# The first two tiles behind each RMS norm are multiplied un-normalised, and the token's factor is applied at their PSUM banks

## The chip, the cores and the metric

The kernel runs as one program on one core of a Trainium2 chip. The time is that of one execution on the device, in microseconds (us). The engines have short names: PE is the matrix engine (TensorE), with PEld its weight loads, DVE is VectorE, ACT is ScalarE, POOL is GpSimd and SP is the queue that issues most DMAs. Each engine runs its own instructions in order, and the engines wait for each other by semaphores. The median of three runs of the kernel before is 3070.98 us (3070.7 to 3072.57).

## What is computed

Two layers of a transformer-like network over 768 tokens of width 1024 (512 latent and 256 context tokens). Each layer is a half SwiGLU, a mixer, and another half SwiGLU. Everything is float32. All three parts begin alike, and this beginning is what the change is about:

```python
def rms_norm(x, g):
    y = xf * lax.rsqrt(jnp.mean(xf * xf, axis=-1, keepdims=True) + EPS)
    return (y * g.astype(F32)).astype(x.dtype)

def _modulate(h, g, m, k):
    return (rms_norm(h, g) * (1 + m[:, :, 3 * k + 1]) + m[:, :, 3 * k]).astype(h.dtype)

def swiglu(h, w1, w3, w2):
    return (jax.nn.silu(h @ w1) * (h @ w3)) @ w2
```

The modulation `m` differs between latent and context tokens. So the input of a product `h @ W` is, for channel d and token t, `x[d,t] * a[d] * r[t] + s[d]`, with `a` the scale (norm weight times 1 + modulation), `r` the token's factor (the inverse root of its mean square) and `s` the shift. The mixers (neighbourhood attention with a state space scan, and a linear recurrence with differential attention) use the same norm ahead of their input product.

## The kernel before

**Layout.** Channels lie on the 128 partitions, in KC = 8 chunks, and tokens along the free axis; `x` holds 8 chunks of 768 tokens. A product is cut in tiles of 128 output channels. A tile's sum lies in `G[0]` or `G[1]` in turn, two PSUM buffers of two banks each; `psum_free[s]` counts when one may be overwritten, `mm_done` counts finished tiles. In the program the tiles are numbered through: ffn0 (60 tiles), ab_in (24), ab_out (8), ffn1, ffn2, cd_in (20), cd_out (8), ffn3. An FFN runs in two halves of 22 "up" tiles (11 pairs of a gate and a hidden tile) and 8 "down" tiles.

**Precision.** Each operand is split in a high part (rounded for the matrix engine's fast float32 format) and a rest. A chunk of a tile is three products: high by high, high by rest, rest by high, each in two matmuls of 384 tokens (lines 428, 430, 432; 512 tokens in one matmul at 435 to 439 where only latent tokens run). The weights' high part is an ACT instruction (`split_hi`, line 890), the rest a DVE one (`split_lo`, line 1299), and both need the buffer `wh`/`wl` of the tile two before to be read out. The activations have `xh` and `xl` likewise.

**A norm.** There are six, numbered 0 to 5: ahead of ffn0, ab_in, ffn1, ffn2, cd_in, ffn3. While the down tiles ahead of it run, DVE adds each to `x`, ACT squares the chunk (957) and POOL adds the squares up (1893). Behind the last tile PE sums over partitions (466, 469) and runs five matmuls whose result nobody uses (475). ACT takes logarithm and exponential (972, 975), which gives `rstd`. Then for each of the 8 chunks: POOL multiplies `x` by `rstd` (1902; chunk 0 is DVE's, 1426), DVE applies scale and shift (1433, one instruction for latent and one for context tokens), ACT rounds the high part (978) and DVE takes the rest (1422). The `gemm_pair` that follows runs the first two tiles together, chunk by chunk, each as soon as its `xl` is there; the third tile's weights are split when the pair has ended.

**The order** of each engine's instructions is the order in which its function calls them. Nothing moves them later. Behind norm 2 the queue of ACT also fetches the modulation's weights (`load_mods`, 896) and the vector `scb` (`load_scb`, 913, 915) ahead of the next weight split. In the "up" part of ffn0 and ffn1, DVE, POOL and ACT compute the modulation from these (1304, 1910, 906), three channels' tiles for each pair.

## Time and profile before

| | us |
|---|---|
| median of 3 runs | 3070.98 |
| the profiled execution | 3072.22 |
| its span on the core | 3069.8 |
| PE busy in it | 2860.1 (93%) |
| DVE, ACT, POOL busy | 1474.5, 1094.9, 646.5 |

The profile shows every instruction of one execution, with its start, its duration and what ended the engine's idle time ahead of it. The span is 2.4 us shorter than the execution's own time. In the names, `tmp` are the buffers of a chunk, `raw` is a weight tile as it was loaded, and L with a number is a line of the kernel.

### The profile page before, as it was taken

How to read it: one execution, taken by the hardware profiler on the slowest of the kernel's cores; microseconds unless marked ns; L12 is line 12 of the kernel's file. 1: busy time of each engine (PE TensorE's matmuls, PEld its weight loads, DVE VectorE, ACT ScalarE, POOL GpSimd, SP SyncE). 2: the span in 40 equal slices, each digit the busy share in tenths (PEclk: the TensorE clock that was granted, in tenths of full speed). 3: DMA queues.
4: the chain of work that ended last, by engine and by line, in shares of the span. 5: the costliest groups of instructions: out<-in, count | busy, mean ns of one | idle time of the engine just before them, and what ended most of it. 6: DMA issues, size and time to landing. Idle time of an engine off the chain costs nothing.

```text
span 3069.8 us, 40707 instructions
## 1 busy us (share of the span) xinstructions
PE 2860.1 (93%) x15782; PEld 2658.3 (87%) x15782; DVE 1474.5 (48%) x1848; ACT 1094.9 (36%) x1465; POOL 646.5 (21%) x336
## 2 busy tenths in 40 slices
PE   5899999989977797999999899999998987899999
PEld 5899999978965687999999899999997855668887
DVE  7874366254556836652564422222225557543332
ACT  3342144125455333431342243112212657454221
POOL 4441144120013714430342300000022113110000
PEclk8999999999999898999999999999999989899999
DMA  6443144111210012441342112211211210123233
GB/s 259 155 147 124 57 158 151 63 43 52 72 38 1 1 42 103 157 154 58 130 157 93 37 62 62 75 55 61 72 51 56 62 55 1 42 75 101 91 96 103
DMA packets 67666, 258.70 MB, mean 84 GB/s; under 512 B 7424, under 2 KB 8576, under 8 KB 66944
## 3 DMA queue, kind: packets, MB, share of 16 engines
q1 hardware_dynamic: 50016, 192.58, 18.9%
q10 hardware_dynamic: 17568, 65.02, 6.0%
q8 instruction: 53, 0.87, 0.1%
q14 instruction: 29, 0.24, 0.0%
HBM read 255.47 MB, written 2.10 MB: 84 GB/s over the span
## 4 chain that ended last, share of the span: by engine, by line
PE 81%; DVE 10%; ACT 2%; issue 2%; POOL 1%; DMA 0%; DVEq 0%; ACTq 0%; POOLq 0%
PE G L428 20%; PE G L432 20%; PE G L430 20%; PE G L435 5%; PE G L439 5%; PE G L437 5%; DVE tmp L1433 2%; DVE B L1304 1%; DVE xl L1422 1%; DVE sL L1632 1%; PE NP L691 1%; PE G L782 1%; DVE wl L1299 1%; DVE sL L1623 1%; PE NP L600 1%
## 5 line engine op out<-in xcount | busy, mean ns | idle before, releaser
L890 ACT ACTIVATE wh<-raw 128x1024 fp32r<-128x1024 f32 (+1 forms) x300 | 338.8, 1129 | 1578.0 <-PE G L432 1285.0
L428 PE MATMUL G<-xh,wh 128*128 128x384 f32 x2752 | 711.3, 339 | 73.4 <-DVE xl L1422 47.7
L430 PE MATMUL G<-xl,wh 128*128 128x384 f32 x2752 | 704.7, 337 | 0.0
L432 PE MATMUL G<-xh,wl 128*128 128x384 f32 x2752 | 704.0, 336 | 0.0
L1299 DVE TENSOR_TENSOR wl<-raw,wh 128x1024 fp32r<-128x1024 f32 (+1 forms) x300 | 429.4, 1431 | 406.8 <-ACT wh L890 406.0
L428 PEld LDWEIGHTS G<-xh,wh 128*128 128x128 f32 x2752 | 500.3, 190 | 87.6 <-issue 40.9
L430 PEld LDWEIGHTS G<-xl,wh 128*128 128x128 f32 x2752 | 503.0, 190 | 0.0
L432 PEld LDWEIGHTS G<-xh,wl 128*128 128x128 f32 x2752 | 501.9, 190 | 0.0
L1910 POOL TENSOR_TENSOR mraw<-mraw,scb 128x1024 f32<-128x1024 f32 x120 | 315.0, 2625 | 598.7 <-DVE B L1304 598.7
L428 PE MATMUL G<-hh,wh 128*128 128x384 f32 x1056 | 268.0, 334 | 0.0
L432 PE MATMUL G<-hh,wl 128*128 128x384 f32 x1056 | 267.8, 334 | 0.0
L430 PE MATMUL G<-hl,wh 128*128 128x384 f32 x1056 | 267.8, 334 | 0.0
L1364 DVE SCALAR_TENSOR_TENSOR x<-G,modG,x 128x256 f32<-128x256 f32 x112 | 49.1, 480 | 440.0 <-PE G L432 440.0
L1304 DVE SCALAR_TENSOR_TENSOR B<-mraw,scb 128x1024 f32<-128x1024 f32 x120 | 235.2, 1960 | 0.0
L435 PE MATMUL G<-xh,wh 128*128 128x512 f32 (+1 forms) x544 | 207.6, 391 | 8.2 <-DVE xl L1422 4.0
L439 PE MATMUL G<-xh,wl 128*128 128x512 f32 (+1 forms) x544 | 205.2, 387 | 0.0
L437 PE MATMUL G<-xl,wh 128*128 128x512 f32 (+1 forms) x544 | 205.1, 387 | 0.0
L1332 DVE TENSOR_TENSOR tmp<-tmp,G 128x768 f32<-128x768 f32 x66 | 63.0, 954 | 295.4 <-PE G L432 294.4
L432 PEld LDWEIGHTS G<-hh,wl 128*128 128x128 f32 x1056 | 190.6, 188 | 0.0
L428 PEld LDWEIGHTS G<-hh,wh 128*128 128x128 f32 x1056 | 190.6, 188 | 0.0
L430 PEld LDWEIGHTS G<-hl,wh 128*128 128x128 f32 x1056 | 190.6, 188 | 0.0
L906 ACT ACTIVATE mraw<-mraw 128x1024 f32<-128x1024 f32 x120 | 126.3, 1053 | 34.4 <-ACT mraw L906 24.0
(308 smaller groups left out, 3104.3 us busy)
## 6 DMA issues: line engine op xcount, KB each, us to landing
raw<-in_w SPq DMA_DIRECT2D x176, 512.0 KB, 3.6
mraw<-in_wmn ACTq DMA_DIRECT2D x120, 512.0 KB, 4.4
raw<-in_w SPq DMA_DIRECT2D x64, 704.0 KB, 4.1
raw<-in_abin SPq DMA_DIRECT2D x24, 512.0 KB, 3.5
raw<-in_cdin SPq DMA_DIRECT2D x20, 512.0 KB, 3.6
mini<-in_wmn SPq DMA_DIRECT2D x9, 512.0 KB, 14.8
gmini<-in_wmn SPq DMA_DIRECT2D x2, 2048.0 KB, 22.0
raw<-in_about SPq DMA_DIRECT2D x8, 512.0 KB, 3.6
```

The lines of the kernel that those rows point to most:

```text
L428: pe.matmul(bank(h), W, tokens(rh, h), start=(k == 0), stop=False)
L430: pe.matmul(bank(h), W, tokens(rl, h), start=False, stop=False)
L432: mm = pe.matmul(bank(h), L, tokens(rh, h), start=False, stop=(k == nk - 1))
L435: pe.matmul(G[slot][:, a:b], W, rh[:, k, a:b], start=(k == 0), stop=False)
L437: pe.matmul(G[slot][:, a:b], W, rl[:, k, a:b], start=False, stop=False)
L439: mm = pe.matmul(G[slot][:, a:b], L, rh[:, k, a:b], start=False, stop=(k == nk - 1))
L890: act.activation(wh[slot][:, 0:nk * P], raw[slot][:, 0:nk * P], ACT.Copy).then_inc(hi_done, 1)
L906: act.activation(mraw[:, j, :], mraw[:, j, :], ACT.Copy, accum_out=M[:, bass.ds(it * 3 + (24 + j), 1), 1:2].rearrange("p a s -> p (a s)")) ...
L1299: dve.tensor_tensor(wl[slot][:, 0:nk * P], raw[slot][:, 0:nk * P], wh[slot][:, 0:nk * P].bitcast(F32), ALU.subtract).then_inc(lo_done, 1)
L1304: return dve.scalar_tensor_tensor(B67[:], tile, 1.0, scv[:, s, :], ALU.mult, ALU.mult, accum_out=out)
L1332: dve.tensor_tensor(by_block(hf[:, 0:T]), by_block(g1s[:, 0:T]), from_banks(G[1], 0, T), ALU.mult).then_inc(psum_free[1], 1)
L1910: pool.tensor_tensor(mraw[:, j, :], mraw[:, j, :], scb[:, 1, :], ALU.mult).then_inc(mod_prod, 1)
```

## The change

For norms 1 to 5 (norm 0 has no product running ahead of it):

- DVE multiplies each chunk of `x` by the scale as soon as the down tile ahead has been added (`ub`), ACT rounds it and DVE takes the rest; this is `unnormed(n)`. Two more columns, the shift for latent and for context tokens, stand behind the 768 tokens of each chunk.
- PE takes the first tile wholly, then the second, on these operands (`gemm_unnormed`), in matmuls of 512 and 258 columns. The norm's sums over partitions stand behind the first tile's third chunk. The five matmuls of line 475 are gone.
- At the bank, DVE copies the two shift columns and multiplies the tokens by `rstd`; the shift's product is added later (`scale_bank` and its callers).
- The norm itself, for all later tiles, runs meanwhile. POOL's multiplication is gone: DVE takes `x * a * rstd` in one instruction for each kind of token, ACT adds the shift as its bias while it rounds, and DVE adds the shift and takes the rest in one. This holds for norm 0, too. The third tile waits for each chunk.
- The modulation of the next norm is prepared ahead of the down tiles. In ffn1, `load_scb` stands behind the first hidden chunk, and the modulation's work starts one pair later.

In the diff, `gemm_unnormed` and what follows it is PE's, the `norm` with `between` ACT's, and from `scale_bank` on it is DVE's (the part with `nn` stands behind the addition of a down tile).

```diff
+            def gemm_unnormed(t, n, segs):
+                uh, ul = (hxh, hxl) if n in (2, 5) else (xh, xl)
+                e = NLAT if segs is SEGS else NLAT // 2
+                ns = segs[-1][1]
+                for s in range(2):
+                    weights_ready(t + s, s, t // 2)
+                    for k in range(KC):
+                        if s == 0:
+                            pe.wait_ge(u_ready, 8 * (n - 1) + k + 1)
...
+                        parts = ((0, e, 0), (512, 512 + ns + 2 - e, e))
+                        for a, b, o in parts:
+                            pe.matmul(G[s][:, a:b], W, uh[:, k, o:o + b - a], start=(k == 0), stop=False)
...
+                        if s == 0 and k == 2:
+                            norm_sums(n, segs)
...
-                    if h == 0:
-                        gemm_pair(b, xh, xl, segs, xn)
-                    with pe.Fori(int(h == 0), FH) as i:
+                    elif h == 0:
+                        gemm_unnormed(b, n, segs)
+                        gemm(b + 2, 0, b // 2 + 1, KC, xh, xl, gsegs, xn)
+                        gemm(b + 3, 1, b // 2 + 1, KC, xh, xl, gsegs)
+                        done = 2
...
             def norm(n, segs, between):
-                    act.wait_ge(aff_done, 8 * n + j + 1)
-                    act.activation(xh[:, j, 0:ns], yn[j % 2][:, 0:ns], ACT.Copy).then_inc(xn_hi, 1)
+                    act.wait_ge(v_ready, 8 * n + j + 1)
+                    if n in IN_PLACE:
+                        if j < KC - 1:
+                            act.wait_ge(u_read, 7 * IN_PLACE.index(n) + j + 1)
...
+                        ins = act.activation(xh[:, j, a:b], vn[j % 4][:, a:b], ACT.Identity, bias=M[:, c0 + j, c:c + 1])
+                    ins.then_inc(xn_hi, 1)
+                    between(j)
+            def between_up(n, segs):
+                def between(j):
+                    if j == 0:
+                        split_hi(FIRST_TILE[n] + 2, 0, FIRST_TILE[n] // 2 + 1, KC)
+                    if j == 3:
+                        act.wait_ge(u_gate, LATE_UP.index(n) + 1)
+                        for a, b, c in segs:
+                            ins = act.activation(g1u[:, a:b], g1u[:, a:b], ACT.Silu, bias=pb[:, 0, c:c + 1])
+                        ins.then_inc(psum_free[0], 1)
...
+            def scale_bank(s, n, ns, out):
+                dve.wait_ge(mm_done, FIRST_TILE[n] + s + 1)
+                dve.tensor_copy(pb[:, s, :], G[s][:, T:TX])
+                for src, a, b in late_tokens(G[s], ns):
+                    ins = dve.tensor_tensor(out[:, a:b], src, rstd[:, a:b], ALU.mult)
+                return ins
+            def scale_gate(n, segs):
+                scale_bank(0, n, segs[-1][1], g1u).then_inc(u_gate, 1)
+                split_lo(FIRST_TILE[n] + 2, 0, KC)
+            def scale_hidden(n, segs):
+                chain(scale_bank(1, n, segs[-1][1], hfu))
+                dve.wait_ge(psum_free[0], FIRST_TILE[n] // 2 + 1)
+                for a, b, c in segs:
+                    ins = dve.scalar_tensor_tensor(hfu[:, a:b], hfu[:, a:b], pb[:, 1, c:c + 1], g1u[:, a:b], ALU.add, ALU.mult)
+                ins.then_inc(psum_free[1], 1)
...
+                        if nn is not None:
...
+                                ins = dve.tensor_scalar(ub[j % 2][:, a:b], x[:, j, a:b], modA[:, nn, j, c:c + 1], None, ALU.mult)
+                            ins.then_inc(u_scaled, 1)
...
-                chain(dve.tensor_tensor(vn[0][:, 0:ns], x[:, 0, 0:ns], rstd[:, 0:ns], ALU.mult))
+                        ins = dve.scalar_tensor_tensor(vn[j % 4][:, a:b], x[:, j, a:b], modA[:, n, j, c:c + 1], rstd[:, a:b],
+                                                       ALU.mult, ALU.mult)
```

Where the instructions stand now, at three places. On PE, from the last down tile of ffn0 to the first tiles of ab_in. Before: the sums, the five matmuls, then the pair, chunk by chunk of both tiles (`wh_57` and `wh_58` are the weights of the two).

```order
L466 MATMUL NP<-ssq,con 128x512
L466 MATMUL NP<-ssq,con 128x256
L469 MATMUL NP<-sq_66,con 128x512
L469 MATMUL NP<-sq_66,con 128x256
L475 MATMUL G<-con 128x512 x5
L428 MATMUL G<-xh,wh_57 128x384 x2
L430 MATMUL G<-xl,wh_57 128x384 x2
L432 MATMUL G<-xh,wl_59 128x384 x2
```

After: the first tile's third chunk ends, the sums follow, and the same tile's fourth chunk goes on.

```order
L507 MATMUL G<-xh,wh_57 128x512
L507 MATMUL G<-xh,wh_57 128x258
L509 MATMUL G<-xl,wh_57 128x512
L509 MATMUL G<-xl,wh_57 128x258
L511 MATMUL G<-xh,wl_59 128x512
L511 MATMUL G<-xh,wl_59 128x258
L488 MATMUL NP<-ssq,con 128x512
L488 MATMUL NP<-ssq,con 128x256
L491 MATMUL NP<-sq_66,con 128x512
L491 MATMUL NP<-sq_66,con 128x256
L507 MATMUL G<-xh,wh_57 128x512
L507 MATMUL G<-xh,wh_57 128x258
```

The sums moved from ahead of the product into its first tile, and the second tile no longer takes turns with it.

On DVE, at norm 1, from the last weight rest on. Before (`tmp_61`, `tmp_62` hold x times rstd, `tmp_63`, `tmp_64` the modulated chunk):

```order
L1299 TENSOR_TENSOR wl_60<-raw_56,wh_58 128x1024
L1318 TENSOR_TENSOR M<-M,par 128x48
L1386 SCALAR_TENSOR_TENSOR modA<-M,par 128x16
L1395 TENSOR_SCALAR modG<-M 128x16
L1426 TENSOR_TENSOR tmp_61<-x,rstd 128x768
L1433 TENSOR_SCALAR tmp_63<-tmp_61,modA,M 128x512
L1433 TENSOR_SCALAR tmp_63<-tmp_61,modA,M 128x256
L1433 TENSOR_SCALAR tmp_64<-tmp_62,modA,M 128x512
L1433 TENSOR_SCALAR tmp_64<-tmp_62,modA,M 128x256
L1422 TENSOR_TENSOR xl<-tmp_63,xh 128x768
```

After (`pb` is the copy of the shift's columns, `vT` the first tile's output, `wl_59` the third tile's weights):

```order
L1590 SCALAR_TENSOR_TENSOR tmp_61<-x,modA,rstd 128x512
L1590 SCALAR_TENSOR_TENSOR tmp_61<-x,modA,rstd 128x256
L1590 SCALAR_TENSOR_TENSOR tmp_62<-x,modA,rstd 128x512
L1590 SCALAR_TENSOR_TENSOR tmp_62<-x,modA,rstd 128x256
L1581 SCALAR_TENSOR_TENSOR xl<-tmp_61,M,xh 128x512
L1581 SCALAR_TENSOR_TENSOR xl<-tmp_61,M,xh 128x256
L1468 COPY pb<-G 128x2
L1470 TENSOR_TENSOR vT<-G,rstd 128x512
L1470 TENSOR_TENSOR vT<-G,rstd 128x256
L1492 TENSOR_SCALAR vT<-vT,pb 128x512
L1492 TENSOR_SCALAR vT<-vT,pb 128x256
L1403 TENSOR_TENSOR wl_59<-raw_55,wh_57 128x1024
```

The first bank's work and the third tile's weight rest now stand between chunk 0's rest and chunk 2, in the middle of the norm.

On ACT, from the end of norm 2 into ffn1. Before:

```order
L978 ACTIVATE xh<-tmp_64 128x768
L896 DMA mraw<-in_wmn 128x1024 x3
L913 DMA scb<-in_ccb 128x2048
L915 ACT_TABLE_LOAD
L915 ACTIVATE scb<-scb 128x2048
L890 ACTIVATE wh_57<-raw_55 128x1024
L924 ACTIVATE tmp_61<-G 128x768
L890 ACTIVATE wh_58<-raw_56 128x1024
```

After (`sq_65` holds the first hidden chunk):

```order
L1064 ACTIVATE xh<-tmp_64,M 128x256
L951 DMA mraw<-in_wmn 128x1024 x3
L945 ACTIVATE wh_58<-raw_56 128x1024
L995 ACTIVATE hh<-sq_65 128x768
L968 DMA scb<-in_ccb 128x2048
L970 ACTIVATE scb<-scb 128x2048
L945 ACTIVATE wh_57<-raw_55 128x1024
L979 ACTIVATE tmp_61<-G 128x768
```

The second weight split and the first chunk's high part moved ahead of the fetch of `scb`; what is queued behind that fetch is now the fifth tile's weights, not the third's.

## Rows read from the trace of the kernel before

**Rows 1.** PE's timeline, norm 1: start, us, line, operation [idle before <-releaser].

```profile
631.14 1.45 PE L466 MATMUL NP<-ssq,con 128*128 128x512 f32 x4
633.54 1.56 PE L469 MATMUL NP<-sq,con 128*128 128x512 f32 x4 [0.95 <-ACT sq L957]
...
645.07 0.98 PE L428 MATMUL G<-xh,wh 128*128 128x384 f32 x2 [5.69 <-DVE xl L1422]
...
668.80 0.62 PE L428 MATMUL G<-xh,wh 128*128 128x384 f32 x2 [1.43 <-DVE wl L1299]
```

**Rows 2.** DVE's timeline in ab_in: copies of two tiles in a row.

```profile
677.46 0.96 DVE L1498 COPY vT<-G 128x768 f32<-128x768 f32 x1 [6.71 <-PE G L432]
...
685.77 0.96 DVE L1498 COPY vT<-G 128x768 f32<-128x768 f32 x1 [5.94 <-PE G L432]
```

**Rows 3.** timeline of DVE at norm 1: weight rest, chunks.

```profile
632.52 1.22 DVE L1299 TENSOR_TENSOR wl<-raw,wh 128x1024 fp32r<-128x1024 f32 x1
...
638.32 2.57 DVE L1426 TENSOR_TENSOR tmp<-x,rstd 128x768 f32<-128x768 f32 x1 [4.16 <-ACT rstd L975]
...
657.71 2.20 DVE L1433 TENSOR_SCALAR tmp<-tmp,modA,M 128x512 f32<-128x512 f32 x2
...
660.89 0.87 DVE L1433 TENSOR_SCALAR tmp<-tmp,modA,M 128x512 f32<-128x512 f32 x2
```

**Rows 4.** timeline of PE, norms 2, 3, 5: first sum, third tile.

```profile
1156.54 1.45 PE L466 MATMUL NP<-ssq,con 128*128 128x512 f32 x4
...
1200.05 1.00 PE L428 MATMUL G<-xh,wh 128*128 128x384 f32 x2 [7.30 <-DVE wl L1299]
...
1734.91 1.45 PE L466 MATMUL NP<-ssq,con 128*128 128x512 f32 x4
...
1773.36 0.62 PE L428 MATMUL G<-xh,wh 128*128 128x384 f32 x2 [2.23 <-ACT tmp L924]
...
2689.16 1.02 PE L466 MATMUL NP<-ssq,con 128*128 128x512 f32 x2
...
2716.49 0.50 PE L435 MATMUL G<-xh,wh 128*128 128x512 f32 x1 [2.38 <-ACT tmp L924]
```

**Rows 5.** ACT's timeline behind norm 2: scb, its Silu, fifth tile's weights.

```profile
1188.51 0.46 ACTq L913 DMA_DIRECT2D scb<-in_ccb  x1
...
1195.80 1.91 ACT L915 ACTIVATE scb<-scb 128x2048 f32<-128x2048 f32 x1 [5.52 <-DMA scb<-in_ccb]
...
1219.27 1.06 ACT L890 ACTIVATE wh<-raw 128x1024 fp32r<-128x1024 f32 x1 [3.61 <-PE G L432]
```

**Rows 6.** timeline of DVE at norm 0: first and last work of the norm.

```profile
52.92 0.96 DVE L1426 TENSOR_TENSOR tmp<-x,rstd 128x768 f32<-128x768 f32 x1
...
74.64 1.96 DVE L1422 TENSOR_TENSOR xl<-tmp,xh 128x768 fp32r<-128x768 f32 x2
```

**Rows 7.** timeline of PE at the third tile of ab_out.

```profile
1106.50 0.62 PE L428 MATMUL G<-xh,wh 128*128 128x384 f32 x2 [1.45 <-DVE wl L1299]
```

**Rows 8.** DVE's groups by shape: xcount | busy us, mean ns | idle.

```profile
L1364 DVE SCALAR_TENSOR_TENSOR x<-G,modG,x 128x256 f32<-128x256 f32 x112 | 49.1, 480 | 440.0 <-PE G L432 440.0
...
L1371 DVE SCALAR_TENSOR_TENSOR x<-G,modG,x 128x512 f32<-128x512 f32 x24 | 18.0, 751 | 100.2 <-PE G L439 100.2
```

**Rows 9.** timeline of ACT at norm 1: the high part of one chunk.

```profile
659.95 0.84 ACT L978 ACTIVATE xh<-tmp 128x768 fp32r<-128x768 f32 x1 [2.33 <-DVE tmp L1433]
```

**Rows 10.** the page's DMA issues: KB each, median us from issue to landing.

```profile
raw<-in_w SPq DMA_DIRECT2D x176, 512.0 KB, 3.6
...
raw<-in_w SPq DMA_DIRECT2D x64, 704.0 KB, 4.1
```

**Rows 11.** timeline of DVE behind norm 5: the fifth tile's weight rest.

```profile
2725.00 1.23 DVE L1299 TENSOR_TENSOR wl<-raw,wh 128x1024 fp32r<-128x1024 f32 x1 [5.76 <-ACT wh L890]
```

**Rows 12.** stretches: us, busy by engine, PEclk, DMA share, GB/s.

```profile
668.80:672.00 3.20, 3.20 (x18) 3.20 (x19) 1.95 (x2) 0.00 (x0) 0.00 (x0) 1.00 0.48 164
...
2718.00:2720.00 2.00, 2.00 (x6) 1.54 (x5) 1.24 (x2) 0.49 (x1) 0.00 (x0) 0.50 0.42 152
```

More of the change, by code:

```diff
@@ L324, in group, with unnormed, shift, late_tokens @@
             return [j in g for g in MINI_GROUPS].index(True)
+        IN_PLACE = (1, 3, 4)
+        LATE_UP = (2, 3, 5)
+        FIRST_TILE = {1: BASE["ab_in"], 2: BASE["ffn1"], 3: BASE["ffn2"], 4: BASE["cd_in"], 5: BASE["ffn3"]}
+        def unnormed(n):
+            return (hxh, hxl) if n in (2, 5) else (xh, xl)
+        def shift(n):
+            c0 = (n // 3) * NMT + 3 * KC * (n % 3)
+            return M[:, c0:c0 + KC, :]
+        def late_tokens(buf, ns):
+            e = NLAT if ns == T else NLAT // 2
+            return ((buf[:, 0:e], 0, e), (buf[:, 512:512 + ns - e], e, ns))
         def by_block(ap):
@@ L933, in pair @@
                         sum_mod(now, 0, more)
+                first = 0
+                if unnormed_first:
+                    split_hi(b + 3, 1, b // 2 + 1, KC)
+                    act.wait_ge(psum_free[1], b // 2 + 1)
+                    act.activation(hh[:, 0, 0:ns], hfu[:, 0:ns], ACT.Copy).then_inc(h_hi, 1)
+                    first = 1
                 if mods is None:
-                    with act.Fori(0, FH - 1) as i:
+                    with act.Fori(first, FH - 1) as i:
                         pair(i, KC)
@@ L939, in up @@
                     return
+                if unnormed_first:
+                    act.wait_ge(h_ready, hb + 1)
+                    load_scb(2)
                 end = mods + FH - 2
                 last = end in (19, 39)
-                pair(0, KC, now=mods)
-                with act.Fori(1, FH - 2) as i:
-                    pair(i, KC, late=i + (mods - 1), now=i + mods)
-                pair(FH - 2, KC, late=end - 1, now=end, more=not last)
-                pair(FH - 1, look, late=end, late_more=not last)
+                pair(first, KC, now=mods)
+                with act.Fori(first + 1, FH - 2 + first) as i:
+                    pair(i, KC, late=i + (mods - 1 - first), now=i + (mods - first))
+                if first:
+                    pair(FH - 1, look, late=end - 1, now=end, more=not last)
+                    sum_mod(end, 1, not last)
+                    sum_mod(end, 2, not last)
+                else:
+                    pair(FH - 2, KC, late=end - 1, now=end, more=not last)
+                    pair(FH - 1, look, late=end, late_more=not last)
             def square(j, n, chunk, ns):
@@ L971, in norm @@
+                            act.activation(uh[:, j, 0:ns], ub[j % 2][:, 0:ns], ACT.Copy).then_inc(u_hi, 1)
+            def norm(n, segs, between):
+                ns = segs[-1][1]
+                c0 = (n // 3) * NMT + 3 * KC * (n % 3)
                 act.wait_ge(norm_sum, n + 1)
-                act.activation(sq[0][:, 0:ns], NP[:, 0:ns], ACT.Ln, bias=eps[:, 0:1], scale=1.0 / D
-                               ).then_inc(norm_ln, 1)
-                act.wait_ge(norm_ln, n + 1)
+                chain(act.activation(sq[0][:, 0:ns], NP[:, 0:ns], ACT.Ln, bias=eps[:, 0:1], scale=1.0 / D))
@@ L1111, in ssd_act @@
                 act.wait_ge(gn_sum, 4)
[L1112 to L1113 removed]
+                chain(act.activation(lng[:], NP[:, 0:T], ACT.Ln, bias=eps[:, 0:1], scale=1.0 / 512))
                 act.activation(rsg[:], lng[:], ACT.Exp, scale=-0.5).then_inc(gn_rs, 1)
@@ L1482, in conv @@
                     ins.then_inc(conv_done, 1)
-                for c in range(AB_IN_T):
+                for c in range(1, AB_IN_T):
                     t, s = AB + c, c % 2
@@ L1707, in conv @@
                     ins.then_inc(conv_done, 1)
-                for c in range(CD_IN_T):
+                for c in range(1, CD_IN_T):
                     t, s = CD + c, c % 2
```

322 lines of the change are left out of this document (188 added, 134 removed).

## The prediction, made before the changed kernel had run

> **What bounds the kernel now.** PE is busy for 93% of the span, so the time lies in its matmuls and in the stretches where it waits. I went first to PE's timeline around a norm, then to DVE's, which PE names as its releaser. At norm 1 the last down tile ends at 631.14; the third tile of ab_in begins at 668.80, 37.66 us later [rows 1]. Two tiles lie between, and a tile costs 8.31 us, the distance of two copies in a row in the steady product [rows 2]. So 37.66 - 16.62 = 21.0 us of each such norm are not product. PE sums for about 2.7 us of them, and waits for the chain Ln, Exp, x times rstd, scale and shift, high part, rest. Then it is paced by that chain: chunk follows chunk at 3.18 us (657.71 to 660.89), where PE needs 2.08 for both tiles. DVE's scale and shift takes 2.20 us there, and 0.87 on the last chunk, when POOL has no multiplication left [rows 3]. After the pair the third tile's weights are late: their releaser is `wl` or the gate's bank [rows 1, 4]. The same distance is 43.51 us at norm 2, 38.45 at norm 3 and 27.33 at norm 5 (512 tokens) [rows 4]; norm 4 repeats norm 1 to 0.1 us. At norm 2 the third tile waits 7.30 us more, since ACT sits behind the load of `scb` (issue 1188.51, Silu 1195.80) [rows 5]. Norm 0 ends on DVE at 76.60, after 23.7 us [rows 6].
>
> **What it becomes, with t = 0 at the end of the last down tile.** I follow norm 1 and give the others by what differs.
>
> PE no longer waits at t = 0. The first tile's weights were split a tile earlier, and its chunks 0 to 6 were rounded under the down tiles. Chunk 7 needs the addition (1.4), the scaling (0.9, as the 0.87 above), the weight rest (1.22) and its own rest (about 1.0): ready at 4.6, wanted after 10. Each down tile gets some 2.2 us more of DVE and 0.8 of ACT, under 8.3 us or more of PE; this costs nothing. An exception is ab_out's third tile, which already waits for its weights' rest [rows 7]: the scaling stands ahead of that, **+1.0 us**. Tile one takes 8.3 + 2.7 for the sums (two groups of four passes, 1.45 and 1.56 us with their drains [rows 1]): it ends at 11.0, tile two at 19.3.
>
> The norm. Its second group of sums starts at 3.1 + 1.3 = 4.4. Between the same point and DVE's first chunk lie 638.32 - 633.54 = 4.78 us before [rows 1, 3], so DVE starts at 9.2. From here DVE decides. A chunk is now two pairs of scalar_tensor_tensor, of 512 and 256 tokens: 0.751 + 0.480 us [rows 8], 1.23 for a pair; two in a row overlap a little, and I take 1.07, with 1.23 as the other bound. That is 2.14 us a chunk instead of 3.18, with no POOL in it. ACT needs two instructions for 0.84 us of work [rows 9], an estimated 0.95, and keeps up.
>
> - Norm 1: ACT must not overwrite chunk 0 before tile two has read it, at 11.0 + 1.0 + 0.2. High part until 13.2, rest until 14.3. The bank (copy 0.1, product 1.0, shift 0.9) and the third tile's weight rest 1.22 make 3.2: 17.5. Then 13 pairs, 13.9: 31.4. Two small instructions 0.4, the second bank and the fourth tile's rest 3.2: the fourth tile begins at **35.1**. PE could have begun it at about 32.5, so DVE still bounds. Before it was 37.66 + 8.31 = 45.97. **-10.9 us**, and the same at norm 4, **-10.8**.
> - Norm 3: the bank's shift is left to ACT, so 2.4 instead of 3.2; 13 pairs end at 30.6. Second bank with the gate's product 2.3, weight rest 1.2: 34.2 against 38.45 + 8.31 = 46.8. **-12.6.** ACT gives the gate's bank back at 23.3, which delays the third tile by 4, but it still ends before DVE does.
> - Norm 2: its operands lie elsewhere, so the high part need not wait; DVE's first rest ends at 12.5, the fourth tile begins at 32.4 and ends at 40.7. The first hidden chunk's rest ends at 33.3, and only then is `scb` fetched. Its landing is not 7.3 us as before, when 1.5 MB were issued right ahead of it: 512 KB take 3.6 us and 704 KB 4.1 [rows 10], from which I estimate 4.9 for 1 MB. Silu 1.9, high part 1.05, rest 1.2: the fifth tile begins at 42.6, a wait of 1.9. Before it began at about 1219.1, 62.6 us behind 1156.54 [rows 4, 5]. **-20.0**; with 7.3 us of landing and a cold start behind the wait it is -15.9.
> - Norm 5: 512 tokens, 0.67 us each instead of a pair, and two matmuls of 256 and 258 columns instead of one, about 5.8 us a tile. The same steps give the fourth tile at 23.5. Before, the third tile ended about 1.3 us ahead of 2725.00 [rows 11], at 34.5. **-11.0.**
> - Norm 0: 14 steps of 1.07 until the last chunk goes to ACT, 67.9 instead of 74.7 (52.92 + 15.0; before, ACT takes it where DVE's last rests begin [rows 6]). All that follows, `scb` included, comes that much earlier: **-6.8.**
>
> The sum is 1.0 - 6.8 - 10.9 - 20.0 - 12.6 - 10.8 - 11.0 = -71.1.
>
> **The clock.** In the row of 2716.49, PE starts the third tile after 2.38 us of idleness, and the granted clock is 0.50 (the 1.2 GHz level) in 2718 to 2720; at norm 1, after 1.43 us behind the weights, it stays at 1.00, 2.4 GHz [rows 4, 12]. The fourth tile will start after 2.1 to 2.6 us of idleness in five places. A cold start costs about 1.7 us: that third tile took 2716.49 to about 2723.7, 7.2 us where its work is 8.31 x 512 / 768 = 5.5 [rows 2, 4, 11]. I charge three of the five, **+5.0**; none or all five move this by -5 and +3.4.
>
> So -66.1 us. From the profiled execution of 3072.22 this gives 3006.1; that execution lay 1.2 us above the median, so I forecast **3005 us**.
>
> A rule speaks against the change. DVE's single-input instruction took 0.87 us for 768 tokens and a two-input one with a scalar takes 1.07 to 1.23 [rows 3, 8]: fusing the product with rstd gives up a fast form. The Trainium skill ("SBUF — State Buffer", "Who interferes with whom") has the other side: DVE's fast single-input form and POOL's reads exclude each other. The rows agree, 2.20 us beside POOL and 0.87 without. By the page alone, the old form without POOL would cost 0.95 + 0.87 + 0.95 a chunk, more than the new 2.14.
>
> **Rivals.**
> 1. *The chunk chain is slower than two pairs.* If each rest waits for ACT's round trip (1.07 + 0.95 + 1.07 and two hand-overs of 0.1, 3.3 us a chunk), seven chunks cost 1.15 more each in six norms: +48, **3053 us**. For it: today's chain waits like this, 3.18 us a chunk. Against: another chunk's pair stands between the two, and four buffers instead of two.
> 2. *PE is cold through the third tiles.* At norms 1 and 4 that tile gets a chunk each 2.14 us for 1.04 us of work. If the clock falls there and behind every wait, all five fourth tiles and norm 2's fifth start cold: **3011 us**, within the range.
> 3. *Slower: the 258-column matmuls.* In the fast float32 format no row shows a width that is no multiple of 128. If such a piece ran at the rate of the sums' plain float32, where 768 columns take about 1.3 us, it would take 0.43 us instead of 0.11. In two tiles of five norms these are 240 pieces of it, 24 a tile: +77, **3082 us**. It decides from about 0.39 us a piece. Against: 256, 384 and 512 columns all cost one column per cycle of 2.4 GHz.
> 4. *The change does not do what it says*, because the fourth tile waits for the same chain that the first waited for. This is half true already, and priced: from t = 0 to the fourth tile there are 35.1 us with 24.9 of product. It would only cancel the gain if DVE had 11 us more in the chain, 0.8 us on each of 13 pairs; no row points there. **3071 us.**
>
> **How the numbers follow.** The forecast's own case holds 0.72, from 2994 (no cold start, a little less on DVE) to 3020 (1.23 us a pair: 16 x 0.16 in six norms is 14). Rival 1 has 0.07, rival 2 0.09, rival 3 0.05, rival 4 0.03, and 0.04 is left for something between. The range 2994 to 3030 holds the forecast, rival 2 and part of the rest, about 0.83. A measurement of this kernel can tell 0.2% (6 us) from no change. Faster: 0.91; same: 0.03, rival 4; slower: 0.06, rival 3 and some unseen cost.
>
> **What the profile of the changed kernel would show.** PE without idle from the last down tile to the end of tile two, 19.3 us; the fourth tile 35.1 us (norm 2: 32.4, norm 3: 34.2, norm 5: 23.5) behind it, with DVE's `wl` as its releaser; pairs of DVE at 1.07 us each; the fifth tile of ffn1 after a wait of about 2 us. I am wrong if the 258-column pieces stand out, if chunks follow each other at over 2.5 us in tile three, if down tiles begin to show gaps, or if the fifth tile of ffn1 waits over 5 us.

## The result, and the profile after the change

The changed kernel takes 3054.4 us (median of four runs, 3051.2 to 3056.7) beside 3071.7 us for the kernel before: 0.995 of the time, 95% interval 0.993 to 0.996. It is faster by 17 us where 66 were forecast, and lies outside the range of 2994 to 3030. The profiled execution took 3056.2 us, with a span of 3054.4.

The page of the changed kernel, the busy times of its engines:

```profile
PE 2886.8 (95%) x15780; PEld 2688.9 (88%) x15780; DVE 1538.8 (50%) x2035; ACT 1084.7 (36%) x1514; POOL 569.8 (19%) x294
```

PE was busy for 2860.1 us before and is for 2886.8 now. The matmuls of the warm-up are gone and nothing large was added to PE, yet it is busy 27 us longer. That is the first sign: time went from waiting into the matmuls.

The places that the forecast spoke of came out as forecast. PE's timeline of the changed kernel (start, duration, instruction, and in brackets the idle time before it with its releaser), at norms 1 to 5:

```profile
635.07 1.45 PE L488 MATMUL NP<-ssq,con 128*128 128x512 f32 x4
...
666.96 0.61 PE L450 MATMUL G<-xh,wh 128*128 128x384 f32 x2 [1.93 <-DVE wl L1403]
...
1160.08 1.45 PE L488 MATMUL NP<-ssq,con 128*128 128x512 f32 x4
...
1189.63 0.62 PE L450 MATMUL G<-xh,wh 128*128 128x384 f32 x2 [1.97 <-DVE wl L1403]
...
1202.06 0.61 PE L450 MATMUL G<-xh,wh 128*128 128x384 f32 x2 [2.06 <-DVE wl L1403]
...
1731.83 1.45 PE L488 MATMUL NP<-ssq,con 128*128 128x512 f32 x4
...
1763.52 0.62 PE L450 MATMUL G<-xh,wh 128*128 128x384 f32 x2
...
2301.87 1.45 PE L488 MATMUL NP<-ssq,con 128*128 128x512 f32 x4
...
2334.41 1.01 PE L450 MATMUL G<-xh,wh 128*128 128x384 f32 x2 [2.17 <-DVE wl L1403]
...
2681.34 1.02 PE L488 MATMUL NP<-ssq,con 128*128 128x512 f32 x2
...
2702.72 0.50 PE L457 MATMUL G<-xh,wh 128*128 128x512 f32 x1 [0.30 <-DVE wl L1403]
```

L488, the first sum, stands behind three chunks of the first tile, 3.17 us behind the end of the last down tile (2.16 with 512 tokens). So t = 0 is 631.90 at norm 1 (631.14 before, [rows 1]), and the fourth tile begins at 666.96, 35.1 us later: the forecast was 35.1. At norm 2 it is 32.7 (forecast 32.4), at norm 3 34.9 (34.2), at norm 4 35.7 (35.1), at norm 5 23.5 (23.5). The releaser is DVE's `wl`, as forecast, except at norm 3, where the fourth tile follows the third without a wait. The fifth tile of ffn1 (1202.06) is later, 45.2 instead of 42.6.

Now lay the starting points of the norms beside each other. Norm 1 starts at 631.90 against 631.14 in [rows 1], though norm 0 ended some 7 us earlier; norm 2 at 1156.9 against 1156.54 in [rows 4], though norm 1 gave its 11 us. What each norm gives, the steady product between two norms takes back. There the groups of PE's instructions by shape (busy us, mean ns of one) read, before the change:

```profile
L428 PE MATMUL G<-xh,wh 128*128 128x384 f32 x2752 | 711.3, 339 | 73.4 <-DVE xl L1422 47.7 <-DVE wl L1299 23.4 <-ACT tmp L924 2.2
L428 PE MATMUL G<-hh,wh 128*128 128x384 f32 x1056 | 268.0, 334 | 0.0
```

and in the changed kernel, where the same matmul is L450:

```profile
L450 PE MATMUL G<-xh,wh 128*128 128x384 f32 x2624 | 694.5, 346 | 39.4 <-DVE wl L1403 18.8 <-DVE xl L1581 14.3 <-issue 6.0
L450 PE MATMUL G<-hh,wh 128*128 128x384 f32 x1056 | 267.9, 334 | 0.0
```

A piece that reads `xh` takes 346 ns in the mean instead of 339; one that reads `hh` takes 334 in both. The change made the rows of `xh` and `xl` two floats longer (770) and left those of `hh`. Windows of PE's activity (busy time with the matmuls counted, granted clock, share of DMA, GB/s), before:

```profile
1900.00:1920.00 20.00, 20.00 (x117) 1.00 0.21 68
2760.00:2780.00 20.00, 20.00 (x90) 1.00 0.30 105
```

and after:

```profile
1900.00:1920.00 20.00, 20.00 (x114) 1.00 0.21 72
2760.00:2780.00 20.00, 20.00 (x88) 1.00 0.32 87
```

PE is fully busy in all four at the full clock, and gets 2 to 3% fewer matmuls done. The timeline shows where: single chunks. Before the change, the first product of two chunks in a row:

```profile
1905.55 0.51 PE L428 MATMUL G<-xh,wh 128*128 128x384 f32 x2
...
1906.59 0.51 PE L428 MATMUL G<-xh,wh 128*128 128x384 f32 x2
```

and after, of three:

```profile
1905.30 0.51 PE L450 MATMUL G<-xh,wh 128*128 128x384 f32 x2
...
1906.34 0.53 PE L450 MATMUL G<-xh,wh 128*128 128x384 f32 x2
...
1907.43 0.52 PE L450 MATMUL G<-xh,wh 128*128 128x384 f32 x2
```

A chunk of three products took 1.04 us each time; now it takes 1.04 and then 1.09. A row of 770 floats is 3080 bytes, so every second chunk begins 8 bytes off a multiple of 16. Over a whole stretch (the 150 us behind the first half of ffn1, the starts of some 850 matmuls, clock 1.00) the eight chunks of a tile take 8.587 us instead of 8.320. L450 counts 2624 pieces, 16 a tile: 164 tiles of 768 tokens, 44 us. The 62 tiles of 512 tokens take 5.574 us instead of 5.440, 8 us more. Together this is a little more than the 49 us that are missing.

### The profile page after: what moved, and what is told of

It reads as the page before. It is cut to its first block, busy times and chain, and to the rows that moved or that the text cites. A ratio compares the mean times of both kernels' runs of the same rounds, so it can differ in the third digit from the quotient of the medians.

```text
span 3054.4 us, 40954 instructions
## 1 busy us (share of the span) xinstructions
PE 2886.8 (95%) x15780; PEld 2688.9 (88%) x15780; DVE 1538.8 (50%) x2035; ACT 1084.7 (36%) x1514; POOL 569.8 (19%) x294
## 4 chain that ended last, share of the span: by engine, by line
PE 83%; DVE 9%; ACT 2%; issue 2%; POOL 1%; DMA 0%; DVEq 0%; ACTq 0%; POOLq 0%
PE G L450 20%; PE G L452 20%; PE G L454 20%; PE G L461 5%; PE G L459 5%; PE G L457 5%; DVE B L1408 1%; DVE xl L1581 1%; DVE sL L1795 1%; DVE wl L1403 1%; PE NP L742 1%; DVE tmp L1590 1%; PE G L846 1%; PE G L833 1%; PE NP L651 1%
## 5 line engine op out<-in xcount | busy, mean ns | idle before, releaser
L450 PE MATMUL G<-xh,wh 128*128 128x384 f32 x2624 | 694.5, 346 | 39.4 <-DVE wl L1403 18.8
L452 PE MATMUL G<-xl,wh 128*128 128x384 f32 x2624 | 689.2, 344 | 0.0
L454 PE MATMUL G<-xh,wl 128*128 128x384 f32 x2624 | 686.3, 343 | 0.0
L1403 DVE TENSOR_TENSOR wl<-raw,wh 128x1024 fp32r<-128x1024 f32 (+1 forms) x300 | 416.8, 1389 | 401.6 <-ACT wh L945 400.6
L450 PEld LDWEIGHTS G<-xh,wh 128*128 128x128 f32 x2624 | 485.2, 191 | 49.8 <-DVE wl L1403 19.9
L452 PEld LDWEIGHTS G<-xl,wh 128*128 128x128 f32 x2624 | 487.9, 191 | 0.0
L454 PEld LDWEIGHTS G<-xh,wl 128*128 128x128 f32 x2624 | 487.0, 190 | 0.0
L450 PE MATMUL G<-hh,wh 128*128 128x384 f32 x1056 | 267.9, 334 | 0.0
L450 PEld LDWEIGHTS G<-hh,wh 128*128 128x128 f32 x1056 | 190.6, 188 | 0.0
```

The costliest lines, as they stand in the source:

```text
L450: pe.matmul(bank(h), W, tokens(rh, h), start=(k == 0), stop=False)
L452: pe.matmul(bank(h), W, tokens(rl, h), start=False, stop=False)
L454: mm = pe.matmul(bank(h), L, tokens(rh, h), start=False, stop=(k == nk - 1))
L1403: dve.tensor_tensor(wl[slot][:, 0:nk * P], raw[slot][:, 0:nk * P], wh[slot][:, 0:nk * P].bitcast(F32), ALU.subtract).then_inc(lo_done, 1)
```

## Experiments

Three theories. **A**: what costs is where the streamed operand's rows start. **B**: what costs is a row length other than 768 floats. **C**: what costs is the changed work itself, the 258-column pieces, more instructions on DVE and ACT, the clock. The last runs ask which part of the change gives the gain. Times are medians, beside runs of the kernel before on the same chip (3071.5 to 3072.9 us).

### Rows of 772 floats in the changed kernel

```diff
-TX = T + 2
+TX = T + 4
...
-                dve.tensor_copy(pb[:, s, :], G[s][:, T:TX])
+                dve.tensor_copy(pb[:, s, :], G[s][:, T:T + 2])
```

> The changed kernel with rows of xh and xl 772 floats long instead of 770 (3088 bytes, a multiple of 16); the two extra columns, the pieces of 258 columns and all else stay. Theory A, the start of the rows: in the changed kernel every second chunk of xh and xl begins 8 bytes off a multiple of 16, and a chunk of three products takes 1.09 us there against 1.05 for its neighbour and 1.04 before the change. A tile loses 0.2 us, some 184 tiles of 768 tokens and the 512-token ones lose 45 to 50 us. Then this kernel takes 3054 - 47 = 3007 us (3002 to 3014), and PE's 20-us windows hold 117 to 118 matmuls again. Theory B, the pitch: any row that is not 768 floats long is slower. Then it stays at 3054. Theory C, the changed work itself (the 258-column pieces, more instructions of DVE and ACT beside PE, the clock): 3054 too.

Measured: 3029.7 us (0.986 of before, 0.984 to 0.987). Chunks take 1.039 to 1.070 us, 8.426 a tile. B and C fall as they stood: two floats more in a row, never read, make the kernel 25 us faster. A's own range, 3002 to 3014, was missed: its first form, multiples of 16 bytes, is too lenient, as half the loss stays. In the tiles of 512 tokens nearly all of it stays, 5.566 us each against 5.574 with rows of 770.

### Rows of 770 floats in the kernel before

```diff
-        xh = at("xh", [P, KC, T], w, F32R); w += KC * T
+        xh = at("xh", [P, KC, T + 2], w, F32R); w += KC * (T + 2)
... (the same for xl; buffers that lie inside the two move with them)
```

> The kernel before, with nothing changed but the length of the rows of xh and xl, 770 floats instead of 768 (the two more are never read). Theories A (start of the rows) and B (pitch): every tile fed by xh and xl loses 0.2 us as in the changed kernel, 3071 + 45 to 50 = 3119 us (3112 to 3126), windows of 113 to 114 matmuls in place of 117 to 118. Theory C (the changed work): 3071.

Measured: 3121.9 us, 49.2 above the kernel before (1.016, 1.014 to 1.018). This is the direct measurement of the step that the forecast left out. Chunk by chunk the two kernels agree: 1.058, 1.087, 1.061, 1.103, 1.047, 1.093, 1.049, 1.090 us here, and 1.057, 1.087, 1.061, 1.102, 1.048, 1.092, 1.049, 1.090 in the changed kernel. Nothing else of the change slows a steady tile, and C has no part in it.

### The kernel before with its buffers shifted by 8, 16, 32 and 64 bytes

The rows stay 768 floats; only the start moves. The shift of 8 bytes (16: `4` for `2`):

```diff
-        xh = at("xh", [P, KC, T], w, F32R); w += KC * T
+        xh = at("xh", [P, KC * T + 8], w, F32R)[:, 2:KC * T + 2].rearrange("p (k t) -> p k t", k=KC); w += KC * T + 8
(the same for xl)
```

> The kernel before, rows of xh and xl 768 floats long as they were, but both buffers begin 2 floats (8 bytes) later, so that every chunk begins 8 bytes off a multiple of 16. Theory A (start of the rows): all eight chunks of a tile cost what every second one does in the changed kernel, 8 x 0.05 = 0.4 us a tile; with 184 tiles and the 512-token ones twice the loss of the changed kernel, 3071 + 80 to 100 = 3161 us (3145 to 3180). Theory B (pitch) and theory C (the changed work): 3071.

> The kernel before, rows of 768 floats, both buffers begin 4 floats (16 bytes) later. Theory A (start of the rows, counted in 16 bytes), B and C: 3071 (3068 to 3075). If what matters is a start counted in 32 or 64 bytes, it is as slow as the one with 8 bytes, 3145 to 3180, and the changed kernel with rows of 772 floats keeps its slow chunks.

For 32 and 64 bytes each buffer is 16 floats longer and the slice begins at 8 or 16:

> The kernel before, rows of 768 floats, both buffers begin 8 floats (32 bytes) later, so that every chunk begins 32 bytes off a multiple of 64. If the start counts in 32 bytes: 3071 (3068 to 3076), a chunk 1.04 us. If it counts in 64 bytes: a chunk of 1.05 to 1.07 us as at 16 bytes off, 3090 to 3115.

> The kernel before, rows of 768 floats, both buffers begin 16 floats (64 bytes) later. If only the start modulo 64 bytes counts: 3071 (3068 to 3075), a chunk 1.04 us. If the shift itself, or the bank that a row falls in, counts: slower, as the shift by 16 bytes was (3115).

As each buffer also grew, `xl` starts 32 bytes further than `xh` modulo 64 in the first two, which their descriptions don't say. Measured, with the time of a chunk in the same stretch:

| shift | `xh`, `xl` start modulo 64 | chunk, 768 tokens, us | chunk, 512 tokens, us | time, us | ratio (95%) |
|---|---|---|---|---|---|
| none | 0, 0 | 1.040 | 0.680 | 3071.7 | |
| 8 bytes | 8, 40 | 1.093 | 0.700 | 3146.5 | 1.024 (1.022 to 1.026) |
| 16 bytes | 16, 48 | 1.067 | 0.700 | 3115.1 | 1.014 (1.012 to 1.016) |
| 32 bytes | 32, 32 | 1.047 | 0.707 | 3090.6 | 1.006 (1.004 to 1.007) |
| 64 bytes | 0, 0 | 1.047 | 0.703 | 3088.7 | 1.005 (1.004 to 1.007) |

PE's timeline with the shift of 8 bytes, the first product of two chunks in a row, 1.09 us apart:

```profile
1520.98 0.53 PE L428 MATMUL G<-xh,wh 128*128 128x384 f32 x2
...
1522.07 0.53 PE L428 MATMUL G<-xh,wh 128*128 128x384 f32 x2
```

And with the shift of 32 bytes, in the tiles of 512 tokens, 0.71 us apart (0.68 unshifted):

```profile
2766.23 0.40 PE L435 MATMUL G<-xh,wh 128*128 128x512 f32 x1
...
2766.93 0.40 PE L435 MATMUL G<-xh,wh 128*128 128x512 f32 x1
```

That the start matters holds, and B falls: the rows have 768 floats in all of them. In the tiles of 768 tokens a chunk pays 0.053 us at 8 bytes and 0.027 at 16. The shift of 16 bytes fell between the times that A foresaw for its two forms (3071, or 3145 to 3180). The expectation for 64 bytes (3071) was missed: 0.007 us a chunk remains there, as much as at 32 bytes. So a start modulo 64 isn't the whole rule, and "only the start modulo 64 counts" is refuted. The tiles of 512 tokens, whose matmuls read 512 tokens in one run and not three blocks of 128, say so more clearly: they pay 0.020 to 0.027 us a chunk for every shift, and 32 bytes cost them more than 8. What orders these prices, and the last 0.007 us, is open.

### The weights shifted by 16 bytes

The tiles fed by `hh` had kept 1.04 us in every kernel, but in all of them `hh` and the weights had moved together. So the distance between streamed rows and loaded weights could have been the cause.

```diff
-        wh = [at(f"wh{s}", [P, FH * P], w + s * FH * P, F32R) for s in range(2)]; w += 2 * FH * P
+        wh = [at(f"wh{s}", [P, FH * P + 8], w + s * (FH * P + 8), F32R)[:, 4:FH * P + 4] for s in range(2)]; w += 2 * (FH * P + 8)
(the same for wl)
```

> The kernel before, xh, xl, hh and hl where they were, but both weight buffers wh and wl (what TensorE loads as weights) begin 16 bytes later. Theory A' (the start of the operand that streams): its address has not moved, a chunk stays at 1.04 us in tiles fed by xh and in those fed by hh, 3071 us (3068 to 3077), unless the load itself slows. Theory R (what counts is the distance between the streamed rows and the weights that are loaded beside them): tiles fed by hh are now as far off as those fed by xh were when these were shifted by 16 bytes; both kinds take 1.06 to 1.07 us a chunk, and the time is 3071 + 45 + 20 = 3135 us (3110 to 3145).

Measured: 3101.6 us (1.010, 1.008 to 1.011), below the range of the one theory and above that of the other. The group of the first product with `hh`:

```profile
L428 PE MATMUL G<-hh,wh 128*128 128x384 f32 x1056 | 269.7, 336 | 0.0
```

336 ns instead of 334, with `hh` on its old place: where the weights lie costs something too. In tiles fed by `xh` a chunk takes 1.051 us in the mean. It isn't even: tiles whose weights lie in the first pair of buffers (16 bytes off a multiple of 64) space their matmuls at some 176 ns, those of the second pair (48 bytes off) at 174, next to 173 before. By distance alone both should be slow, since the shift by 16 bytes had `xh` 16 and `xl` 48 bytes off with both slow. So distance alone falls, and the loaded operand's own place counts. In tiles of 768 tokens it counts less than the streamed one's. In those of 512 tokens a chunk takes 0.694 us with either pair, beside 0.680.

### Rows of 784 floats in the changed kernel

3136 bytes are 49 x 64. A table product had to move to make room.

```diff
-TX = T + 2
+TX = T + 16
...
-        t2b = small("t2b", [P, NLAT])
+        t2b = at("t2b", [P, NLAT], H + 38 * NLAT); fw[0] += P
```

> The changed kernel with rows of xh and xl 784 floats long (3136 bytes, 49 x 64), so that every chunk begins on a multiple of 64 bytes; to make room the table product of the rotary step lies in another buffer. Rows of 770 floats gave 3054, of 772 3030. Theory A', the start of the rows counted in 32 or 64 bytes (a chunk takes 1.04 us on a multiple of 64, 1.07 at 16 bytes off it in every chunk of the kernel before shifted by 16 bytes, 1.09 at 8 bytes off): all chunks take 1.04 again and what the wider rows cost, 0.24 us in each of some 184 tiles and about 5 in those of 512 tokens, is back: 3054 - 49 = 3005 us (3000 to 3011), the forecast. Theory B (pitch: any row that is not 768 floats long is slower): between 3025 and 3054. Theory C (part of the missing gain is in the changed work itself): 3015 to 3030, with windows of 117 to 118 matmuls and the remainder at the norms.

Measured: **3015.3 us** (3012.3 to 3017.2; 0.981 of before, 0.980 to 0.983), better than both kernels, but above the 3000 to 3011 of theory A' and at the lower end of what theory C foresaw. The tiles tell the two apart. PE's timeline at the norms (L489 is the first sum):

```profile
627.54 1.45 PE L489 MATMUL NP<-ssq,con 128*128 128x512 f32 x4
...
659.41 0.62 PE L451 MATMUL G<-xh,wh 128*128 128x384 f32 x2 [0.72 <-DVE wl L1404]
...
1143.64 1.45 PE L489 MATMUL NP<-ssq,con 128*128 128x512 f32 x4
...
1705.52 1.45 PE L489 MATMUL NP<-ssq,con 128*128 128x512 f32 x4
...
1737.19 0.62 PE L451 MATMUL G<-xh,wh 128*128 128x384 f32 x2 [0.92 <-DVE wl L1404]
...
2265.72 1.45 PE L489 MATMUL NP<-ssq,con 128*128 128x512 f32 x4
...
2640.41 1.02 PE L489 MATMUL NP<-ssq,con 128*128 128x512 f32 x2
```

With 3.13 us taken off each (2.16 for the last), the norms start at 624.4, 1140.5, 1702.4, 2262.6 and 2638.2, and the span ends at 3012.9. Stage by stage against the kernel before:

| from, to | forecast, without clock | rows of 770 | rows of 784 |
|---|---|---|---|
| start to norm 1 | -6.8 | +0.8 | -6.7 |
| norm 1 to norm 2 | -9.9 | -0.4 | -9.3 |
| norm 2 to norm 3 | -20.0 | -6.6 | -16.5 |
| norm 3 to norm 4 | -12.6 | -1.0 | -10.8 |
| norm 4 to norm 5 | -10.8 | -2.7 | -7.6 |
| norm 5 to the end | -11.0 | -5.4 | -6.0 |

A tile takes 8.347 us, 0.027 above 8.320, which leaves 4 to 5 us in all. The stage behind norm 5 gains hardly more than with 770 (-6.0 and -5.4). The fourth tile begins where it should, so the tiles of 512 tokens are still slow: they take 5.56 us each, beside 5.44 before and 5.57 with 770, some 7 us over the 62 of them, though every row starts on a multiple of 64 bytes. So what is missing lies in the steady tiles and not in the changed work, which theory C had named.

### The two columns in a buffer of their own

Rows of 768 floats again; the shift's columns are multiplied by themselves.

```diff
-                        parts = ((0, e, 0), (512, 512 + ns + 2 - e, e))
+                        parts = ((0, e, 0), (512, 512 + ns - e, e))
...
+                        pe.matmul(G[s][:, sa:sb], W, shh[:, k, :], start=False, stop=False)
+                        pe.matmul(G[s][:, sa:sb], W, shl[:, k, :], start=False, stop=False)
...
+                        pe.matmul(G[s][:, sa:sb], L, shh[:, k, :], start=False, stop=False)
```

> The changed kernel with rows of xh and xl 768 floats long, as before the change; the two columns for the shift stand in a buffer of their own and are multiplied by three more matmuls of 2 columns on each chunk of the first two tiles behind norms 1 to 5 (24 a tile, 240 in all), and the pieces of 258 columns become 256. Theory A'' (each operand's own start): all chunks of the other tiles take 1.04 us again, so the 49 us of the 770-float rows come back, and the 8 to 9 us that the rows of 784 floats still miss against the forecast as well, less what the 2-column matmuls cost: between 0.03 and 0.10 us each, 0.7 to 2.4 us a tile, of which the second tile's share is partly under the chain of DVE that bounds: 5 x 1 to 5 x 4 = 5 to 20. 3005 + 5 to 20 = 3010 to 3025 us. If something else in the changed work slowed the tiles, it stays near 3030 or above.

Measured: 3016.6 us (0.982, 0.981 to 0.984), no different from rows of 784. Steady tiles are back at 1.04 us a chunk, those of 512 tokens at 0.68, and the 20-us window of the latter holds 90 matmuls. PE's timeline of the first tile behind norm 1 and of the fourth:

```profile
624.65 0.51 PE L510 MATMUL G<-xh,wh 128*128 128x512 f32 x2
624.99 0.17 PE L511 MATMUL G<-shh,wh 128*128 128x2 f32 x1
...
626.02 0.52 PE L510 MATMUL G<-xh,wh 128*128 128x512 f32 x2
...
662.62 0.75 PE L452 MATMUL G<-xh,wh 128*128 128x384 f32 x2 [1.98 <-DVE wl L1409]
```

A chunk takes 626.02 - 624.65 = 1.37 us instead of 1.04, so each matmul of 2 columns costs 0.11, a little over what was expected. The fourth tile begins 38.0 us behind the last down tile instead of 35.1. With 3.0 more at each of norms 1, 3 and 4, 1.7 at norm 5 and nothing at norm 2, where the fifth tile begins no later than with rows of 784, this is 10.7: taken off 3016.6, it gives 3006, next to the forecast of 3005. The two columns have a price either way, and the forecast had them for nothing.

### The fused chain alone

The kernel before, with the new form of a norm's chunk and nothing hidden:

```diff
-                        ins = dve.tensor_scalar(yn[j % 2][:, a:b], vn[j % 2][:, a:b], modA[:, n, j, c:c + 1],
-                                                M[:, c0 + j, c:c + 1], ALU.mult, ALU.add)
-                    ins.then_inc(aff_done, 1)
+                        ins = dve.scalar_tensor_tensor(tmp[j % 4][:, a:b], x[:, j, a:b], modA[:, n, j, c:c + 1], rstd[:, a:b],
+                                                       ALU.mult, ALU.mult)
+                    ins.then_inc(v_ready, 1)
...
-                pool.wait_ge(rstd_ready, n + 1)
-                for j in range(1, KC):
...
```

> The kernel before with one part of the change alone: the norm's chunk is two pairs of scalar_tensor_tensor (x times scale times rstd, then shift minus high part) in four buffers, and GpSimd multiplies nothing; every tile still waits for the norm, rows stay 768 floats. Theory F (the chain is the larger part): at norm 1 the chain of 16 pairs of 1.07 us starts 7.2 us behind the last down tile and ends at 24.5, the third tile's weight rest 1.2 follows, so that the third tile begins at 26 to 28 instead of 37.66: -10 us at each of norms 1 to 4, -5 at norm 5 (512 tokens, 0.67 us a piece), -7 at norm 0, together -52: 3071 - 52 = 3019 us (3012 to 3030). Theory H (the hiding of the two tiles is the larger part, as the change is described): the chain gives the 1.05 us a chunk on seven chunks only until PE's own 2.08 us a chunk bounds, -5 at each norm, about 3045 us.

Measured: 3028.7 us (0.986, 0.984 to 0.988), 43.6 below the kernel before and already 26 below the changed kernel. DVE's timeline at norm 1:

```profile
633.50 1.14 DVE L1436 SCALAR_TENSOR_TENSOR tmp<-x,modA,rstd 128x512 f32<-128x512 f32 x2
634.56 1.14 DVE L1427 SCALAR_TENSOR_TENSOR xl<-tmp,M,xh 128x512 fp32r<-128x512 f32 x2
635.62 1.14 DVE L1436 SCALAR_TENSOR_TENSOR tmp<-x,modA,rstd 128x512 f32<-128x512 f32 x2
```

and PE's:

```profile
622.85 1.45 PE L466 MATMUL NP<-ssq,con 128*128 128x512 f32 x4
...
652.23 0.61 PE L428 MATMUL G<-xh,wh 128*128 128x384 f32 x2 [1.42 <-DVE wl L1302]
```

A pair takes 1.06 us, a chunk 2.12 instead of 3.18. The third tile begins 29.4 us behind the last down tile (26 to 28 were expected) instead of 37.66 ([rows 1]). Norm 0 ends 7.6 us earlier, at 69.0 instead of 76.6. The chain is the larger part of the gain, as theory F said.

### The hiding alone, with the old chain

The kernel with rows of 784 floats, with the product on GpSimd, scale and shift, and rest as before:

```diff
-                        ins = dve.scalar_tensor_tensor(vn[j % 4][:, a:b], x[:, j, a:b], modA[:, n, j, c:c + 1], rstd[:, a:b],
-                                                       ALU.mult, ALU.mult)
-                    ins.then_inc(v_ready, 1)
+                        ins = dve.tensor_scalar(yn[j % 2][:, a:b], vn[j % 2][:, a:b], modA[:, n, j, c:c + 1],
+                                                M[:, c0 + j, c:c + 1], ALU.mult, ALU.add)
+                    ins.then_inc(aff_done, 1)
```

> The changed kernel with aligned rows (784 floats, 3015 us), but with the norm's chunks as before the change: the product with rstd on GpSimd, scale and shift, high part and rest, in two buffers each. The hiding of the first two tiles stays, the fused chain goes. Chunks follow each other at 3.18 us again instead of 2.12. Theory F: the fourth tile begins 8 x 1.05 = 8.4 us later at norms 1 to 4, 5 later at norm 5, and norm 0 ends 7 later: 3015 + 46 = 3061 us (3052 to 3070), hardly below the kernel before. Theory H: the longer chain is partly hidden under the two tiles, 3035 us.

Measured: 3048.5 us (0.992, 0.991 to 0.994), 33 above the kernel with the fused chain, between the two theories. DVE's timeline at norm 1 and PE's first sum and fourth tile:

```profile
651.28 0.86 DVE L1591 TENSOR_SCALAR tmp<-tmp,modA,M 128x512 f32<-128x512 f32 x2
...
653.12 2.19 DVE L1591 TENSOR_SCALAR tmp<-tmp,modA,M 128x512 f32<-128x512 f32 x2
...
656.28 2.18 DVE L1591 TENSOR_SCALAR tmp<-tmp,modA,M 128x512 f32<-128x512 f32 x2
```

```profile
635.63 1.45 PE L491 MATMUL NP<-ssq,con 128*128 128x512 f32 x4
...
671.84 0.62 PE L453 MATMUL G<-xh,wh 128*128 128x384 f32 x2 [0.77 <-DVE wl L1404]
```

Chunks follow at 3.16 us. But while DVE takes the first tile from its bank, GpSimd multiplies ahead, and one chunk's scale and shift is done in 0.86 us. Also, the fused chain stands still for 2.34 us at its first chunk, until ACT may overwrite what the first tile reads, and the slower one does not. So the fourth tile comes at 39.3 us, 4.3 later and not 8.4. Norm 0, where nothing hides the chain, ends 7.6 us later, as expected. Together: the chain gives 44 us alone and 33 on top of the hiding; the hiding gives 24 alone and 13 on top of the chain. Both figures of the hiding still carry the some 10 us that rows of 784 cost.

### The product on DVE, unfused

```diff
+                    chain(dve.tensor_tensor(vn[j % 2][:, 0:ns], x[:, j, 0:ns], rstd[:, 0:ns], ALU.mult))
...
-                    pool.tensor_tensor(vn[j % 2][:, 0:ns], x[:, j, 0:ns], rstd[:, 0:ns], ALU.mult
-                                       ).then_inc(v_ready, 1)
```

> The kernel before with one step moved: the product x times rstd of a norm's chunk is done by DVE itself (0.95 us) and not by GpSimd; scale and shift, high part and rest stay as they were, in two buffers. Theory P (DVE's scale and shift takes 2.20 us only because GpSimd multiplies beside it, 0.87 without): a chunk is 0.95 + 0.87 + 0.95 = 2.8 us on DVE instead of 3.18, if the round trip of ACT lies beside the next chunk's product: 8 x 0.4 = 3 us less at norms 0 to 4, less at norm 5: 3071 - 15 = 3056 us (3050 to 3062), against 3029 for the fused form. Theory Q (it is slow for another reason, or the round trip of ACT sets the pace): a chunk is 0.95 + 2.20 + 0.95 = 4.1 us, 3071 + 5 x 7 = 3106 us (3095 to 3115).

Measured: 3052.1 us (0.994, 0.992 to 0.995). DVE's timeline at norm 1, one chunk and the product of the next:

```profile
645.13 0.96 DVE L1429 TENSOR_TENSOR tmp<-x,rstd 128x768 f32<-128x768 f32 x1
646.12 0.87 DVE L1431 TENSOR_SCALAR tmp<-tmp,modA,M 128x512 f32<-128x512 f32 x2
...
647.90 0.96 DVE L1429 TENSOR_TENSOR tmp<-x,rstd 128x768 f32<-128x768 f32 x1
```

Theory P holds: with GpSimd silent the scale and shift takes 0.87 us on every chunk, and a chunk 647.90 - 645.13 = 2.77 us, the sum that the forecast had worked out. Taking work from GpSimd onto a DVE that is the bound made the kernel 19 us faster. Still, two fused pairs (2.12) beat three cheap instructions (2.77).

## Why the forecast was wrong, point by point

- **The step that failed: wider rows.** The change part names 258-column pieces, and rival 3 looked at them as a width. The same edit makes the rows 770 floats long for every tile that reads `xh` or `xl`, and that had no term. The forecast left the steady tiles at their old 8.31 us; they took 8.587, and the price, measured alone in the kernel before, is 49.2 us. Forecast 3005 + 49 = 3054, the measured time. That this meets to the microsecond is partly luck, since two smaller terms below were off, one up and one down.
- **Rival 3** did not happen: the 258-column pieces take 283 ns in the mean, with their drains, where those of 256 took 279 to 281. The right kind of cost was weighed at the wrong place. It looked at the width of an instruction and not at where its operand starts.
- **The norms** were right: fourth tile at 35.1, 32.7, 34.9, 35.7 and 23.5 us against 35.1, 32.4, 34.2, 35.1 and 23.5. A pair took 1.06 us against 1.07. With rows of 784 the stage up to norm 1 gave -6.7 against -6.8, the next, with norm 1 and ab_out, -9.3 against -9.9. One reading was loose and did no harm: the third tile of norm 2 waited 7.30 us in all, not 7.30 more than the others; the sum used the distance of 43.51, which is right. **Rivals 1 and 4** are out: a chunk takes 2.12 us, not 3.3, and the fourth tile is not 11 us late.
- **The landing of `scb`** was mis-sized, as the two rows of ACT's queue and ACT in the changed kernel show:

```profile
1190.48 0.33 ACTq L968 DMA_DIRECT2D scb<-in_ccb  x1
1197.80 1.92 ACT L970 ACTIVATE scb<-scb 128x2048 f32<-128x2048 f32 x1 [8.48 <-DMA scb<-in_ccb]
```

  It takes 7.3 us, as in [rows 5], and not the 4.9 estimated from smaller transfers. The fifth tile of ffn1 began at 45.2 instead of 42.6. The other bound, -15.9, is near the -16.5 that this stage gave with rows of 784, but it held a cold start behind that wait, which did not come; the slow stretch lay in the fourth tile instead.
- **The clock.** Three cold starts were charged to fourth tiles. Windows in the changed kernel, in order of time: the fourth tiles of norms 1 and 2, the fifth of norm 2, the fourth of norm 4 (us, PE busy with its matmuls counted, granted clock, DMA share, GB/s):

```profile
668.00:672.00 4.00, 4.00 (x16) 0.57 0.74 232
1190.00:1194.00 4.00, 4.00 (x16) 0.58 0.72 244
1202.00:1206.00 4.00, 3.94 (x22) 1.00 0.46 131
2334.00:2338.00 4.00, 3.59 (x12) 0.57 0.49 150
```

  Three fourth tiles did run partly at the 1.2 GHz level. But so did the third tiles of norms 1, 3, 4 and 5, which had no charge: **rival 2** was partly right about them, and wrong about all five fourth tiles and the fifth. With rows of 784 only one fourth tile (norm 2) had such a stretch, and again four third tiles. The stages with rows of 784 sum to -56.9. The forecast's -71.1, with 9 to 12 for what such rows still cost and 2.5 for `scb`, makes -59.6 to -56.6. At most 3 us are left for the clock where 5.0 were charged; no run measures that term alone.
- **The spread.** The range ended at 3030 as every unknown in it was one of the norm. A cost on each of some 230 steady tiles had no place in it, so one missed step outweighed all the others.

## What to carry to other kernels

When a buffer's rows grow, price it for everything that reads the buffer, not for the code that wanted the columns: here two floats a row cost 49 us over the whole kernel and took three quarters of the gain. Measure the padding alone first. Here rows on a multiple of 64 bytes gave back four fifths of that cost, and only rows of the old length brought every steady tile back to its old time. Before hiding a chain under other work, shorten it: the fused pair gave 44 us without moving a single tile, and the hiding 13 on top, with the price of its wider rows in it.
